# Dilated attention heads regrouped by residue modulo 4: 100 tile pairs a head in place of 136

## The chip, the cores and the metric

One core of one Trainium2 chip runs the whole program in one launch. The metric is the device time in microseconds (us), the median of the runs shown. The engines are TensorE (PE, with its weight loads listed as PEld), VectorE (DVE), ScalarE (ACT), GpSimd (POOL) and SyncE (SP, which issues most DMAs).

## What is computed

The reference is one inference step of a two-layer decoder trunk for a prompt of 2048 tokens and 8 samples of 4 tokens (T = 2048, 32 sample rows, D_MODEL 1024, heads of 128 columns, all fp32). Layer 0 has gated DeltaNet and retention heads. Layer 1 has 4 forgetting-attention heads (C) and 4 dilated ALiBi heads (D). The part that matters here is what a D head does to the prompt:

```python
D_BRANCHES = ((128, 1), (512, 4), (2048, 16))      # window, dilation
parts = [band_branch(dq, dk, dv, slopes, dil, win // dil) for win, dil in D_BRANCHES]
o_d = merge_branches(parts)     # one softmax over the keys of all three branches
# band_branch: s = q.k - slope * distance for distance = 0, dil, 2*dil, ... win, causal
o = concat([o_c * silu(cg), o_d * silu(dg)]);  y = o @ w_out;  x + y
```

So a query at position t sees every key at distance 0 to 128, every fourth key up to 512, and every sixteenth key up to 2048. A key that two or three branches hold counts two or three times. Everything beyond distance 128 lies at a distance divisible by 4, so on keys of the query's own residue modulo 4. `k` and `v` of the prompt are outputs too.

## The kernel before, in words

`build` runs stages one after another: tokens are loaded and turned, the heads of layer 0 (`heads_A`, `heads_B`), `output_projection`, then `odd_heads` (line 1433), then `finish` (line 1836), which does the attention of the samples and the last output projection. The change touches `shape_constants` (line 49) and `odd_heads` alone.

`odd_heads` has one in-order program for each engine, tied by semaphores, and each runs over the 8 heads `u`: four C, then four D. For a head the order written by hand is this:

- **Projection.** `project(u, at)` (L1554) is called for 20 values of `at` (4 matrices in 5 chunks of 416 tokens). DVE takes each chunk from PSUM into `Q` (L1680). `Q[:, 0]` holds the queries with the features on the partitions, `Q[:, 1]` the keys, `Q[:, 2]` the values, `Q[:, 3]` the gate. From `at > 3 * NC` on, `turn_kv(u, g)` (L1570) turns keys and values into rows and DVE keeps them in `ktok` and `vtok` (L1690).
- **Rows.** The prompt is 16 rows `i` of 128 queries. Row i has i + 1 key tiles, in chunks of up to G = 4 tiles (512 keys, one PSUM bank). A tile pair is one tile of 128 queries against one of 128 keys. A head has 1 + 2 + ... + 16 = 136 pairs in 40 chunks.
- **Scores.** `scores(u, i, ch)` (L1578): 128 queries stationary, up to 512 keys moving. An fp32 matmul stands as two MATMUL instructions in the trace.
- **Softening.** `soften` on DVE (L1708) adds the bias row, writes the scores to one of three row slots (`slots`, two in `sc`, one in `Q[:, 2]`, the values being in `vtok` by then) and takes the maximum. `maximum` (L1713, L1714) closes the row. `soft` on ACT (L1777) takes the exponential of the row in place and its sum.
- **Turning.** `turn` (L1592): each 128x128 tile of the row is transposed into PSUM bank 4 or 5. DVE copies chunks 0 and 1 to `wt` (L1746), ACT chunks 2 and 3 (L1804).
- **Weighing.** `weigh` (L1603): `wt` stationary, `vtok` moving, accumulated in bank 6 or 7. DVE divides (`otok`, L1752), PE turns the result (`turn_output`, L1612), and DVE multiplies it by the gate into `O` (L1758, semaphore `o_done`).

Elsewhere in the kernel, `finish` has eight transposes (L1966) whose source is read with a step of 4 fp32 elements, 16 bytes.

The rows are pipelined two ahead. The PE loop of a row is:

```python
for step in range(steps(i)):
    if i + 2 < TILES and step < n_chunks[i + 2]: scores(u, i + 2, step)
    if step == 0: pe.wait_ge(s["exp_done"], TILES * u + i + 1)
    if step < n_chunks[i]: turn(u, i, step)
    if 1 <= step <= n_chunks[i]: weigh(u, i, step - 1)
    if step == 1 and i: turn_output(u, i - 1)
```

DVE goes through the same steps: `soften(i + 2, step)`, the copy of chunk `step` of row i, at step 0 the division of row i - 1, at step 2 its product with the gate, at the end `maximum(i + 2)`. After row 3 comes `keep_sample` (L1697, L1699), which saves the samples' columns. ACT does `soft(i + 1)`, then its copies of row i.

The SP queue loads the bias of a head (`bias`, 2048 columns) when the scores of the head before are kept, then the weights of the next head, then stores keys, values and, when `o_done` says so, rows 0 to 13 and rows 14 and 15 of `O`. POOL multiplies each set of weights by the norm's gain when they have landed (L1522), which falls into the attention part of each head but the last.

Of the kernel before, what the change touches and what calls it, by code (L numbers as in the profile page):

```python
# [19 lines left out]
X = mybir.AxisListType.X  # L20
# [29 lines left out]
def shape_constants():  # L50
# [51 lines left out]
    m = np.arange(T)  # L102
    window = np.stack([bias(i[:, None] + (T - P) - m[None, :], h) for h in range(H)]).astype(f)
# [19 lines left out]
RET = 324  # L123

# [1308 lines left out]
def odd_heads(nc, k, io):  # L1433

    with ExitStack() as c:
# [15 lines left out]
        slots = [sc[:, 0, :], sc[:, 1, :], Q[:, 2, 0:T]]  # L1451
        names = ["fw_loaded", "fw_scaled", "f_ready", "f_taken", "f_act", "f_dve", "f_turned", "cols_ready", "f_stored", "cols_stored",
# [8 lines left out]
        def weights(u):  # L1461
# [4 lines left out]
        n_chunks = [i // G + 1 for i in range(TILES)]  # L1466
        first = [sum(n_chunks[:i]) for i in range(TILES)]
        in_chunk = lambda i, ch: min(G, i + 1 - G * ch)
        by_v, by_s = sum(min(n, 2) for n in n_chunks), sum(max(n - 2, 0) for n in n_chunks)
        CHUNKS = sum(n_chunks)  # L1470

        kept_by = lambda u, i, ch: ("wt_kept_v", by_v * u + sum(min(n, 2) for n in n_chunks[:i]) + ch + 1) if ch < 2 else \
            ("wt_kept_s", by_s * u + sum(max(n - 2, 0) for n in n_chunks[:i]) + ch - 1)
        steps = lambda i: max(n_chunks[i] + 1, n_chunks[i + 2] if i + 2 < TILES else 0, 3)
        stores = lambda u: 16 * sum(4 + (2 if branch == "C" else 2 * B) for branch, h in HEADS[:u])

# [4 lines left out]
        def _(sp):  # L1481
# [43 lines left out]
        def _(pe):  # L1525
# [32 lines left out]
            def turn_kv(u, g):  # L1558
# [5 lines left out]
                for which in range(2):  # L1564
# [6 lines left out]
                    last.then_inc(s["kv_turned"], 1)  # L1571

            def scores(u, i, ch):
                if i and ch < n_chunks[i - 1]:
                    pe.wait_ge(s["scores_kept"], CHUNKS * u + first[i - 1] + ch + 1)
                j, n = G * ch, in_chunk(i, ch) * P
                diag = HEADS[u][0] == "C" and ch == n_chunks[i] - 1
                last = pe.matmul(k.ps[ch][:, 0:n], Q[:, 0, i * P:(i + 1) * P], Q[:, 1, j * P:j * P + n], start=True, stop=not diag)  # L1578
                if diag:
                    last = pe.matmul(k.ps[ch][:, n - P:n], k.c("ident"), k.c("causal_bias"), start=False, stop=True)  # L1580
                last.then_inc(s["scores_made"], 1)

            def turn(u, i, ch):

                at = first[i] + ch
                if at >= 2:
                    i2 = i if ch >= 2 else max(x for x in range(i + 1) if first[x] <= at - 2)
                    name, count = kept_by(u, i2, at - 2 - first[i2])
                    pe.wait_ge(s[name], count)
                for jj in range(in_chunk(i, ch)):  # L1590
                    j = G * ch + jj
                    last = pe.transpose(k.ps[4 + at % 2][:, jj * P:(jj + 1) * P], slots[i % 3][:, j * P:(j + 1) * P], k.c("ident"))  # L1592
                last.then_inc(s["wt_made"], 1)

            def weigh(u, i, ch):

                name, count = kept_by(u, i, ch)
# [3 lines left out]
                for jj in range(in_chunk(i, ch)):  # L1601
                    j = G * ch + jj
# [869 lines left out]
```

## Time and profile before

| | us |
|---|---|
| median of 3 runs | 4541.89 (4537.42 to 4545.32) |
| the profiled execution | 4539.22 |
| its span, first to last instruction | 4537.4 |
| `odd_heads`, the four C heads | about 2101.8 to 2960 |
| `odd_heads`, the four D heads | about 2960 to 3812 |
| `finish` | about 3815 to the end |

Over the span PE is busy 91%, PEld 56%, DVE 38%, ACT 21% and POOL 3%; the mean granted TensorE clock is 0.951 of full speed. All times inside a profile are counted from the start of its span. The span is 1.8 us shorter than the execution's own time, and that execution is 2.7 us below the median. Each D head is a projection of about 124.5 us followed by an attention part of about 88 us. PE, DVE and ACT rows give busy time. An instruction that waits for a semaphore is not busy, and consecutive matmuls overlap: the start of one to the start of the next is what one costs.

### The profile page before, as it was taken

What the parts mean: (1) busy time and instruction counts of PE and PEld (TensorE: products, weight loads), DVE (VectorE), ACT (ScalarE), POOL (GpSimd) and SP (SyncE); (2) the same over time, 40 slices, a digit from 0 to 9 for tenths busy, and PEclk for the clock granted to TensorE, in tenths of its full rate; (3) what the DMA queues carried; (4) which work ended last, traced back from release to release, by engine and by line L of the source; (5) the groups of instructions that cost most, each with busy time, mean ns of one, the idle gap of its engine ahead of it and who ended that gap; (6) DMA issues with size and microseconds to landing.
All of it is one profiled execution on the core that took longest, in us unless ns stands there. A gap on an engine that the chain in (4) does not pass through costs nothing. (4 is left out here: it accounts for less than half of the span.)

```text
span 4537.4 us, 59156 instructions
## 1 busy us (share of the span) xinstructions
PE 4114.4 (91%) x23986; PEld 2525.4 (56%) x23986; DVE 1740.9 (38%) x3961; ACT 961.5 (21%) x1526; POOL 146.1 (3%) x67
## 2 busy tenths in 40 slices
PE   5899989999899999799999999999999997889896
PEld 2475665857555555454565666656565655444443
DVE  2364554647221222212334241515151425444442
ACT  2232332323110110112222222222222222000111
POOL 0000000000000000000000000000000000000000
PEclk7899999999899999899999999999999998999897
DMA  4001020100615523300101010101010102789886
GB/s 106 10 6 43 6 43 5 20 24 6 187 34 164 177 75 113 115 31 10 38 19 38 19 38 19 38 19 48 9 57 15 42 19 86 262 293 312 288 286 223
DMA packets 250756, 379.32 MB, mean 84 GB/s; under 512 B 23369, under 2 KB 154766, under 8 KB 247786
## 3 DMA queue, kind: packets, MB, share of 16 engines
q1 hardware_dynamic: 190358, 185.86, 14.5%
q10 hardware_dynamic: 51408, 157.31, 10.2%
q0 software_dynamic: 8720, 32.38, 2.1%
q8 instruction: 191, 3.13, 0.3%
q14 instruction: 79, 0.65, 0.0%
HBM read 327.90 MB, written 114.56 MB: 98 GB/s over the span
## 5 line engine op out<-in xcount | busy, mean ns | idle before, releaser
L475 PE MATMUL ps<-xT,big 128*128 128x416 f32 x2560 | 909.5, 517 | 15.6 <-PEq L143 9.4
L1554 PE MATMUL ps<-xT,big 128*128 128x416 f32 x2560 | 902.2, 512 | 0.0
L475 PEld LDWEIGHTS ps<-xT,big 128*128 128x128 f32 x2560 | 490.9, 192 | 431.2 <-issue 425.0
L1554 PEld LDWEIGHTS ps<-xT,big 128*128 128x128 f32 x2560 | 483.8, 190 | 397.0 <-issue 396.9
L1680 DVE TENSOR_TENSOR big<-ps,rstd 128x416 f32<-128x416 f32 x160 | 94.7, 592 | 801.1 <-PE ps L1554 801.1
L1603 PE MATMUL ps<-vtok,wt 128*128 128x128 f32 x2176 | 297.0, 280 | 31.9 <-DVE wt L1746 30.9
L2055 PE MATMUL ps<-o_words,big 128*128 128x512 f32 x512 | 286.2, 648 | 27.7 <-DVE xT L2203 13.9
L1578 PE MATMUL ps<-big 128*128 128x512 f32 (+3 forms) x640 | 289.7, 534 | 6.5 <-DVE vtok L1690 6.5
L1603 PEld LDWEIGHTS ps<-vtok,wt 128*128 128x128 f32 x2176 | 264.9, 192 | 53.8 <-DVE wt L1746 51.5
L1375 PE MATMUL ps<-big,wout 128*128 128x416 f32 x640 | 226.5, 516 | 19.1 <-DMA big<-scr_o 19.1
L2146 DVE STREAM_TRANSPOSE big<-rstd 128x512 f32<-128x512 f32 x312 | 207.1, 691 | 62.0 <-DMA rstd<-in_cache_fox_k 47.2
L490 DVE TENSOR_TENSOR big<-ps,rstd 128x416 f32<-128x416 f32 x100 | 59.1, 591 | 447.1 <-PE ps L475 446.9
L1777 ACT ACTIVATE sc<-sc,stat 128x128 f32<-128x128 f32 (+10 forms) x88 | 103.7, 1179 | 430.0 <-DVE stat L1714 430.0
L1375 PEld LDWEIGHTS ps<-big,wout 128*128 128x128 f32 x640 | 122.5, 192 | 122.5 <-issue 102.7
L1708 DVE CUSTOM_DVE_ANT_0 sc<-ps,bias 128x512 f32<-128x512 f32 (+3 forms) x216 | 130.3, 603 | 108.0 <-PE ps L1578 84.6
L1746 DVE COPY wt<-ps 128x512 f32<-128x512 f32 (+1 forms) x224 | 140.9, 629 | 34.4 <-PE ps L1592 34.4
L2029 PE MATMUL ps<-vring,big 128*4 128x128 f32 x2496 | 123.5, 286 | 30.1 <-issue 17.4
L1592 PEld LDWEIGHTS ps<-pack,sc 128*128 128x128 f32 x728 | 91.1, 142 | 80.2 <-issue 71.4
L2261 ACT COPY srow<-ps 128x1024 f32<-128x1024 f32 (+1 forms) x40 | 39.6, 991 | 438.5 <-PE ps L1990 438.5
L684 PE MATMUL ps<-big 128*128 128x128 f32 x896 | 130.9, 288 | 1.6 <-DVE grp L905 0.2
L2055 PEld LDWEIGHTS ps<-o_words,big 128*128 128x128 f32 x512 | 80.6, 194 | 92.1 <-issue 77.9
L2029 PEld LDWEIGHTS ps<-vring,big 128*4 128x4 f32 x2496 | 40.2, 84 | 162.8 <-issue 136.5
(403 smaller groups left out, 4690.9 us busy)
## 6 DMA issues: line engine op xcount, KB each, us to landing
rstd<-in_cache_fox_k SPq DMA_DIRECT2D x256, 256.0 KB, 4.2
vring<-in_cache_fox_v ACTq DMA_DIRECT2D x256, 256.0 KB, 4.5
out_win_k_sample<-in_cache_win_k ACTq DMA_DIRECT2D x8, 4088.0 KB, 28.8
out_win_v_sample<-in_cache_win_v ACTq DMA_DIRECT2D x8, 4088.0 KB, 40.7
big<-in_w_in_even SPq DMA_DIRECT2D x32, 512.0 KB, 10.7
big<-in_w_in_odd SPq DMA_DIRECT2D x32, 512.0 KB, 6.9
o_words<-scr_o POOLq DMA_DIRECT2D x8, 2048.0 KB, 11.5
rstd<-in_cache_win_k SPq DMA_DIRECT2D x56, 256.0 KB, 6.0
```

What stands on the lines that cost most here:

```text
L475: last = pe.matmul(k.ps[banks[at % 2]][:, 0:CH], k.w[:, j, m * P:(m + 1) * P], k.xT[:, j, n * CH:(n + 1) * CH], start=(j == 0), stop=(j == ...
L684: last = pe.matmul(dst, lhs[0:w, sl[i]], rhs[0:w, sl[i]], start=True, stop=True)
L1375: last = pe.matmul(k.ps[at % 4][:, 0:CH], wout[:, j, m * P:(m + 1) * P], o[:, n % 2, j, :], start=(j == 0), stop=(j == KT - 1))
L1554: last = pe.matmul(k.ps[PBANK[at % 2]][:, 0:CH], k.w[:, j, m * P:(m + 1) * P], k.xT[:, j, n * CH:(n + 1) * CH], start=(j == 0), stop=(j == ...
L1578: last = pe.matmul(k.ps[ch][:, 0:n], Q[:, 0, i * P:(i + 1) * P], Q[:, 1, j * P:j * P + n], start=True, stop=not diag)
L1603: last = pe.matmul(k.ps[6 + i % 2][:, 0:P], wt[:, (first[i] + ch) % 2, jj * P:(jj + 1) * P], vtok[:, j, :], start=(j == 0), stop=(j == i))
L1708: dve.tensor_tensor_reduce(slots[i % 3][:, j * P:j * P + n], k.ps[ch][:, 0:n], bias[:, at:at + n], 1.0, -3e38, ALU.add, ALU.max, cmax[:, i ...
L1746: dve.tensor_copy(wt[:, at % 2, 0:n], k.ps[4 + at % 2][:, 0:n]).then_inc(s["wt_kept_v"], 1)
L1777: act.activation(slots[i % 3][:, 0:n], slots[i % 3][:, 0:n], ACT.Exp, bias=stat[:, i % 3, 0:1], accum_out=stat[:, i % 3, 1:2]).then_inc(s[ ...
L2029: last = pe.matmul(k.ps[4][32 * hh:32 * hh + L, 0:P], weights[:, L * hh:L * hh + L], rows[:, hh * P:(hh + 1) * P], start=first, stop=final)
L2055: last = pe.matmul(k.ps[7], wout[:, unit, j, :], o[:, j, :], start=(j == 0), stop=(j == KT - 1))
L2146: dve.transpose(kt[:, at % 2, p % PAGES, :], kring[:, it % RING, :]).then_inc(s["k_turned"], 1)
```

## The change

Only the D heads change what they do. A row `i` is now the 128 queries of residue `i % 4` of the block of 512 tokens number `i // 4` (`tokens(u, i)`, a slice with step 4). It has one chunk or two:

- chunk 0 (near): the 512 keys of its own block, 4 tiles;
- chunk 1 (far, from row 4 on): for each earlier block its 128 keys of the same residue, but for the block just before, whose keys of that residue and whose last 128 keys in a row both stand. That is `i // 4 + 1` tiles.

The tiles of a head are 4 x 4 + 4 x 6 + 4 x 7 + 4 x 8 = 100, in 28 chunks. Score banks alternate between even and odd rows. The three row slots are 1024 wide and all lie in `sc`. Chunk 1 is copied by ACT, chunk 0 by DVE. In `turn_kv`, for g = 0, 1, 2, four more transposes turn the values by residue into bank 4, and DVE copies them to `Q[:, 2]`. The bias comes as two tables, `bias` (2048 columns) and `near` (515 columns, in `sc`), by two DMAs, and SP waits for `wt_made` of the head before as well. `O` is stored as rows 0 to 11 and 12 to 15. For the C heads the same functions give the same instructions as before, with that one more wait in SP.

```diff
+    window = np.zeros((H, P, WINDOW_COLS), f)       # WINDOW_COLS = T + 515
...
-        slots = [sc[:, 0, :], sc[:, 1, :], Q[:, 2, 0:T]]
...
+        TILES_OF = {"C": [[min(G, i + 1 - G * ch) for ch in range(i // G + 1)] for i in range(TILES)],
+                    "D": [[G] if i < G else [G, i // G + 1] for i in range(TILES)]}
+        by_act = lambda u, ch: ch >= (2 if HEADS[u][0] == "C" else 1)
...
+        steps = lambda u, i: max(n_chunks(u, i) + 1, n_chunks(u, i + 2) if i + 2 < TILES else 0, 3)
+        bank = lambda u, i, ch: ch if HEADS[u][0] == "C" else 2 * (i % 2) + ch
+        row_slots = {"C": [sc[:, 0, :], sc[:, 1, :], Q[:, 2, 0:T]],
+                     "D": [sc[:, 0, 0:T // 2], sc[:, 0, T // 2:T], sc[:, 1, 0:T // 2]]}
+        near = sc[:, 1, T // 2:T // 2 + 515]
+        def tokens(u, i):
+            if HEADS[u][0] == "C":
+                return slice(i * P, (i + 1) * P)
+            return slice(512 * (i // 4) + i % 4, 512 * (i // 4 + 1), 4)
...
                 if u:
-                    sp.wait_ge(s["scores_kept"], CHUNKS * u)
-                src = io.scr_f[h:h + 1, :].broadcast_to([P, T]) if fox else io.c_window[h:h + 1].rearrange("o p n -> (o p) n")
-                sp.dma_start(bias, src).then_inc(s["bias_loaded"], 16)
+                    sp.wait_ge(s["scores_kept"], before(u))
+                    sp.wait_ge(s["wt_made"], before(u))
+                if fox:
+                    sp.dma_start(bias, io.scr_f[h:h + 1, :].broadcast_to([P, T])).then_inc(s["bias_loaded"], 16)
+                else:
+                    sp.dma_start(bias, io.c_window[h, :, 0:T]).then_inc(s["bias_loaded"], 16)
+                    sp.dma_start(near, io.c_window[h, :, T:]).then_inc(s["bias_loaded"], 16)
...
-                for a, b in ((0, TILES - 2), (TILES - 2, TILES)):
+                for a, b in ((0, TILES - 2), (TILES - 2, TILES)) if fox else ((0, TILES - 4), (TILES - 4, TILES)):
...
+                if HEADS[u][0] == "D" and g < 3:          # in turn_kv, PE
+                    if g or u > H:
+                        pe.wait_ge(s["vs_kept"], 3 * (u - H) + g)
+                    for r in range(4):
+                        last = pe.transpose(k.ps[4][:, r * P:(r + 1) * P], Q[:, 2, 512 * g + r:512 * (g + 1):4], k.c("ident"))
+                    last.then_inc(s["vs_turned"], 1)
 
             def scores(u, i, ch):
+                fox = HEADS[u][0] == "C"
+                old = i - (1 if fox else 2)
+                if old >= 0 and ch < n_chunks(u, old):
+                    pe.wait_ge(s["scores_kept"], before(u) + first(u, old) + ch + 1)
+                out, q = k.ps[bank(u, i, ch)], Q[:, 0, tokens(u, i)]
...
+                elif ch == 0:
+                    at = 512 * (i // 4)
+                    last = pe.matmul(out, q, Q[:, 1, at:at + 512], start=True, stop=True)
+                else:
+                    at = 512 * (i // 4)
+                    pe.matmul(out[:, 0:n - P], q, Q[:, 1, i % 4:at:4], start=True, stop=True)
+                    last = pe.matmul(out[:, n - P:n], q, Q[:, 1, at - P:at], start=True, stop=True)
...
+            def values(u, i, ch, jj):
+                if HEADS[u][0] == "C":
+                    return vtok[:, G * ch + jj, :]
+                ab, r = divmod(i, 4)
+                if ch == 0:
+                    return vtok[:, 4 * ab + jj, :]
+                if jj == ab:
+                    return vtok[:, 4 * ab - 1, :]
+                return Q[:, 2, 512 * jj + r * P:512 * jj + (r + 1) * P]
...
+                if u >= H:                                # PE, before the rows
+                    pe.wait_ge(s["vs_kept"], 3 * (u - H + 1))
...
+                if HEADS[u][0] == "D" and g < 3:          # in keep_kv, DVE
+                    dve.wait_ge(s["vs_turned"], 3 * (u - H) + g + 1)
+                    dve.tensor_copy(Q[:, 2, 512 * g:512 * (g + 1)], k.ps[4]).then_inc(s["vs_kept"], 1)
...
-                at = j * P + (0 if HEADS[u][0] == "C" else T - (i + 1) * P)
+                if HEADS[u][0] == "C":                    # in soften, DVE
+                    add = bias[:, j * P:j * P + n]
+                elif ch == 0:
+                    add = near[:, 3 - i % 4:3 - i % 4 + n]
+                else:
+                    add = bias[:, 512 * (i % 4 + 1) - n:512 * (i % 4 + 1)]
...
-                            dve.tensor_tensor(O[:, (i - 1) * P:i * P], k.ps[6 + (i - 1) % 2][:, P:2 * P], Q[:, 3, (i - 1) * P:i * P],
+                            dve.tensor_tensor(O[:, tokens(u, i - 1)], k.ps[6 + (i - 1) % 2][:, P:2 * P], Q[:, 3, tokens(u, i - 1)],
                                               ALU.mult).then_inc(s["o_done"], 1)
...
-                    for ch in range(2, n_chunks[i]):
+                    for ch in range(n_chunks(u, i)):      # ACT
+                        if not by_act(u, ch):
+                            continue
```

## Rows read from the trace of the kernel before

**Rows 1.** The page: busy time, share of the span, instructions of each engine.

```profile
PE 4114.4 (91%) x23986; PEld 2525.4 (56%) x23986; DVE 1740.9 (38%) x3961; ACT 961.5 (21%) x1526; POOL 146.1 (3%) x67
```

**Rows 2.** Busy time by stretch: a projection, then the attention parts of four D heads.

```profile
core 0: us, PE busy (x) PEld busy (x) DVE busy (x) ACT busy (x) POOL busy (x), PEclk, DMA share, GB/s
3599.40:3723.90 124.50, 122.33 (x367) 66.84 (x366) 20.51 (x32) 23.68 (x27) 0.00 (x0) 1.00 0.03 10
3084.30:3173.10 88.80, 82.82 (x514) 62.10 (x515) 55.65 (x193) 25.98 (x42) 7.02 (x1) 0.98 0.20 59
3297.10:3385.20 88.10, 81.41 (x514) 61.46 (x515) 56.12 (x193) 25.98 (x42) 7.02 (x1) 1.00 0.20 59
3509.20:3599.90 90.70, 82.94 (x515) 62.34 (x515) 57.54 (x193) 25.98 (x42) 7.02 (x1) 0.98 0.20 58
3723.90:3811.50 87.60, 81.09 (x512) 61.09 (x512) 55.64 (x193) 25.98 (x42) 0.00 (x0) 1.00 0.12 36
```

**Rows 3.** Waits in the D heads: us in total, times, longest.

```profile
PE ps L1603 <- DVE wt L1746: 17.1, 28, 1.9
```

**Rows 4.** Timeline of PE, last D head: start, us, line, count, idle before.

```profile
3727.69 0.91 PE L1578 MATMUL ps<-big 128*128 128x384 f32 x2 [0.81 <-DVE vtok L1690]
...
3735.77 1.02 PE L1578 MATMUL ps<-big 128*128 128x512 f32 x2
...
3738.19 1.16 PE L1603 MATMUL ps<-vtok,wt 128*128 128x128 f32 x8 [0.52 <-DVE wt L1746]
3739.18 0.27 PE L1612 MATMUL ps<-pack,otok 128*128 128x128 f32 x1
3739.29 1.02 PE L1578 MATMUL ps<-big 128*128 128x512 f32 x2
...
3747.54 1.02 PE L1578 MATMUL ps<-big 128*128 128x512 f32 x2
3748.40 0.60 PE L1592 MATMUL ps<-pack,sc 128*128 128x128 f32 x4
3748.84 1.02 PE L1578 MATMUL ps<-big 128*128 128x512 f32 x2
...
3754.86 1.06 PE L1603 MATMUL ps<-vtok,wt 128*128 128x128 f32 x8
3755.75 0.27 PE L1612 MATMUL ps<-pack,otok 128*128 128x128 f32 x1
...
3798.38 1.04 PE L1592 MATMUL ps<-pack,big 128*128 128x128 f32 x8
3799.76 1.16 PE L1603 MATMUL ps<-vtok,wt 128*128 128x128 f32 x8 [0.35 <-DVE wt L1746]
...
3808.34 2.00 PE L1603 MATMUL ps<-vtok,wt 128*128 128x128 f32 x16
```

**Rows 5.** Timeline of DVE, last D head: the last product with the gate.

```profile
3811.22 0.29 DVE L1758 TENSOR_TENSOR big<-ps,big 128x128 f32<-128x128 f32 x1 [0.42 <-PE ps L1612]
```

**Rows 6.** Timeline of ACT, last D head: an exponential and a copy.

```profile
3747.47 1.15 ACT L1777 ACTIVATE sc<-sc,stat 128x1024 f32<-128x1024 f32 x1 [2.74 <-DVE stat L1714]
...
3807.21 0.59 ACT L1804 COPY wt<-ps 128x512 f32<-128x512 f32 x1 [4.01 <-PE ps L1592]
```

**Rows 7.** Timeline at half clock: contiguous scores, contiguous transposes, transposes with step 4.

```profile
3090.46 1.92 PE L1578 MATMUL ps<-big 128*128 128x512 f32 x2
3092.17 0.63 PE L1592 MATMUL ps<-pack,sc 128*128 128x128 f32 x2
...
3822.80 1.98 PE L1966 MATMUL ps<-pack,vring 128*128 128x128 f32 x8 [4.82 <-DMA vring<-in_cache_fox_logf,pages_col]
```

**Rows 8.** Timeline of the third D head: POOL's scaling of weights, DVE's `keep_sample`.

```profile
3520.12 7.02 POOL L1522 TENSOR_TENSOR big<-big,g_odd 128x4096 f32<-128x4096 f32 x1 [206.31 <-DMA big<-in_w_in_odd]
...
3525.30 2.04 DVE L1697 COPY wins<-big 128x32 f32<-128x32 f32 x3
```

**Rows 9.** DMA issues: count, KB each, median us to landing.

```profile
rstd<-in_cache_fox_k SPq DMA_DIRECT2D x256, 256.0 KB, 4.2
```

More of the change, by code:

```diff
@@ L123 @@
 RET = 324
+WINDOW_COLS = T + 515
 def window_rows():
@@ new lines, in odd_heads, with kept_by @@
+        pairs = [PAIRS[branch] for branch, h in HEADS]
+        before = lambda u: sum(len(p) for p in pairs[:u])
+        by_act = lambda u, ch: ch >= (2 if HEADS[u][0] == "C" else 1)
+        n_chunks = lambda u, i: len(tiles_of[u][i])
+        first = lambda u, i: pairs[u].index((i, 0))
+        def kept_by(u, at):
+            who = by_act(u, pairs[u][at][1])
+            earlier = [(v, ch) for v in range(u) for _, ch in pairs[v]] + [(u, ch) for _, ch in pairs[u][:at + 1]]
+            return "wt_kept_s" if who else "wt_kept_v", sum(by_act(v, ch) == who for v, ch in earlier)
@@ L1571, in turn_kv @@
                     last.then_inc(s["kv_turned"], 1)
-            def scores(u, i, ch):
[L1574 to L1580, printed above, removed]
+                if HEADS[u][0] == "D" and g < 3:
+                    if g or u > H:
+                        pe.wait_ge(s["vs_kept"], 3 * (u - H) + g)
+                    for r in range(4):
+                        last = pe.transpose(k.ps[4][:, r * P:(r + 1) * P], Q[:, 2, 512 * g + r:512 * (g + 1):4], k.c("ident"))
+                    last.then_inc(s["vs_turned"], 1)
@@ L1581, in scores @@
                 last.then_inc(s["scores_made"], 1)
             def turn(u, i, ch):
-                at = first[i] + ch
+                at = first(u, i) + ch
                 if at >= 2:
-                    i2 = i if ch >= 2 else max(x for x in range(i + 1) if first[x] <= at - 2)
-                    name, count = kept_by(u, i2, at - 2 - first[i2])
+                    name, count = kept_by(u, at - 2)
                     pe.wait_ge(s[name], count)
-                for jj in range(in_chunk(i, ch)):
+                for jj in range(tiles_of[u][i][ch]):
@@ L1600, in weigh @@
                     pe.wait_ge(s["otok_ready"], TILES * u + i - 1)
-                for jj in range(in_chunk(i, ch)):
-                    j = G * ch + jj
-                    last = pe.matmul(k.ps[6 + i % 2][:, 0:P], wt[:, (first[i] + ch) % 2, jj * P:(jj + 1) * P], vtok[:, j, :],
-                                     start=(j == 0), stop=(j == i))
-                if ch == n_chunks[i] - 1:
+                n, final = tiles_of[u][i][ch], ch == n_chunks(u, i) - 1
+                for jj in range(n):
+                    last = pe.matmul(k.ps[6 + i % 2][:, 0:P], wt[:, at % 2, jj * P:(jj + 1) * P], values(u, i, ch, jj),
+                                     start=(ch + jj == 0), stop=(final and jj == n - 1))
+                if final:
                     last.then_inc(s["o_made"], 1)
@@ L1738, in _ @@
                 for i in range(TILES + 1):
[L1739 to L1740 removed]
+                    for step in range(steps(u, i) if i < TILES else 3):
+                        if i + 2 < TILES and step < n_chunks(u, i + 2):
                             soften(u, i + 2, step)
[L1742 to L1745 removed]
+                        if i < TILES and step < n_chunks(u, i) and not by_act(u, step):
+                            at = first(u, i) + step
+                            n = tiles_of[u][i][step] * P
+                            dve.wait_ge(s["wt_made"], before(u) + at + 1)
                             dve.tensor_copy(wt[:, at % 2, 0:n], k.ps[4 + at % 2][:, 0:n]).then_inc(s["wt_kept_v"], 1)
```

69 lines of the change are left out of this document (35 added, 34 removed).

## The prediction, made before the changed kernel was run

> **What bounds the kernel now.** I read the page first: PE is busy 91% of the span, the other engines far less [rows 1]. Only D heads change, so I then cut that stretch into projection and attention. A D head's projection is 124.5 us at full clock, PE busy all but 2 us of it and DVE busy 20.5. Its attention part is 87.6 to 90.7 us, PE busy 81 to 83 and DVE 56 [rows 2]. So PE bounds both parts, and work taken from PE should show nearly whole, as long as no chain through DVE or ACT takes its place. The waits show how near such a chain is: PE's weighing waited 17.1 us in the four heads for DVE's copy of the transposed tiles, 28 times, so in early rows above all [rows 3]. Last I walked the rows of the last D head on PE's timeline [rows 4].
>
> **Price of a tile pair on PE,** from start to start [rows 4]. Scores: two matmuls of 512 columns from 3747.54 to 3748.40, 0.86 us for four tiles, 0.215 a tile. Turning: four transposes from 3748.40 to 3748.84, 0.44, so 0.109. Weighing: eight matmuls from 3754.86 to 3755.75, 0.89, so 0.223. Together 0.547 us a pair. 36 pairs fewer is 19.7 us a head; what replaces them decides the rest.
>
> **The floor of a row.** Call S0 the near scores of row i + 2, T0 and T1 the transposes of row i, W0 and W1 its weighing. When PE has little between S0 and W0, W0 waits for S0, then the softening, then the copy by DVE: S0 at 3735.77, W0 at 3738.19, 2.42 us. A W0 that has waited takes 0.99 (3738.19 to 3739.18), and turning the last output 0.11 (to 3739.29); this row took 3.52 [rows 4]. In the new D rows every near chunk has four tiles, so this floor holds in all of them. A row costs max(2.42, 0.86 + 0.44 + S1 + T1) + W0 + 0.11 + W1, with W0 0.99 after a wait and 0.89 without. The far chunk of n tiles has S1 0.215n, T1 0.109n, W1 0.223n.
> - Rows 0 to 3 (no far chunk): 3.41 for row 0, which has no output to turn, 3.52 for each other; 13.97.
> - Rows 4 to 7 (2 far tiles, and 2 or 3 scored ahead): PE reaches W0 at 1.95 or 2.16, under 2.42. 3.52 + 0.45 = 3.97 each; 15.88.
> - Rows 8 and 9 (3, scoring 3): 2.27, still under. 4.19 each. Rows 10 and 11 (3, scoring 4): 2.49, no wait, 4.16 each. Together 16.70.
> - Rows 12 and 13 (4, scoring 4): 2.60 + 1.00 + 0.89 = 4.49 each; 8.98.
> - Rows 14 and 15 score nothing. The W0 of such a row starts 1.38 after its first transpose (3798.38 to 3799.76). 1.38 + 0.99 + 0.11 + 0.89 = 3.37 each; 6.74.
> - Tail: the last weighing starts at 3808.34, 16 x 0.112 later is 3810.13 [rows 4], and the last product ends at 3811.51 [rows 5]: 1.38.
>
> Sum 63.65 us. The same stretch before is 3727.69 to 3811.51, 83.8 us [rows 4, 5]. Saved: 20.15 a head.
>
> **What is added in a head.** Twelve transposes of values beside the projection, 12 x 0.109 = 1.31. Row 0 scores four tiles in place of one there, 3 x 0.215 = 0.64. PE is full in that part, so both count [rows 2]. Row 1 scores four tiles in place of two just before the rows, and its softening is longer: 0.4 (bounds 0.3 to 0.7). Sum 2.35; net 17.8 a head, 71.2 for four.
>
> **At nothing.** Three more DVE copies a head, of the size of those DVE makes there, lie in a projection where DVE is busy 20.5 of 124.5 us [rows 2]. ACT takes far copies of 256 to 512 columns: each takes 0.59 at most [rows 6]. In row 14 weighing could start 1.38 - 0.44 = 0.94 after the last transpose, with a copy by DVE between; the same after T1 is covered by W0 and the output, 0.89 + 0.11 = 1.00. ACT's exponential of the next row, 1024 columns there as here, took 1.15 and began at 3747.47, as PE began its row at 3747.54 [rows 4, 6]. So it is over long before T1 ends, 1.95 to 2.6 into the row. DVE's product with step 4 takes 0.29 now [rows 5]; twice that would delay only an exponential needed a row later. In SP, the wait for `wt_made` stands behind a wait for `o_done` of the same head, which comes later; behind it are the bias loads (some 0.26 MB more for `near`) and the next weights. The bias is asked for a projection ahead, over 100 us; if that cover failed, a landing of some 4 us would show [rows 9]. The last store of `O` is 256 KB in place of 128 KB, open at the end of the stage: 0.3 us, bounds 0 and 4.2 [rows 9].
>
> **Disturbances before.** The attention parts of the other three D heads are 1.2, 0.5 and 3.1 us above the last one's [rows 2]. In the third, POOL scales weights from 3520.12 to 3527.14, and DVE's three copies of `keep_sample`, starting at 3525.30, took 2.04 in all and ended with POOL [rows 8]; half clock followed. PE's projection ended at 3509.2, so POOL ended 17.9 us after it. The new rows reach `keep_sample` some 4.2 + 13.97 = 18.2 us after the projection, where before it was 16.1. So it should come just behind POOL: 3.6 us back in two heads. The half clock of the first D head I leave.
> The Trainium skill ("SBUF — State Buffer", Who interferes with whom) says that a DVE copy using both ports and a GpSimd instruction exclude each other for the whole instruction. The trace agrees; if the order came out the other way, it would give those 3.6 us back and perhaps as much again.
>
> **The sum.** 71.2 + 3.6 - 0.3 = 74.5 us. The profiled execution took 4539.2, its span 4537.4; less 74.5 is 4464.7. It lay 2.7 below the median of 4541.9, so the median after is 4467.
>
> **Unknown: operands with step 4.** No matmul of this trace has its moving operand with a step. Below 1 time the contiguous price is excluded, as 0.427 us for 512 columns is already the full clock's pace. The nearest row above is the same matmul at half clock, two in 1.92 against 1.02, start to start twice as long [rows 4, 7]. For a stationary operand there is a row: at half clock two contiguous transposes take 0.63, so eight at twice 0.109 apart would take 0.63 + 6 x 0.218 = 1.94, and eight with step 4 took 1.98 [rows 7]. So the load costs nothing there, and I take 1 time for both. At full clock the twelve transposes could still be held at twice 0.109: 1.3 a head, 5 us.
>
> **Rivals.**
> 1. *The strided keys stream at half pace.* For: nothing in the trace shows full pace. Against: the free stationary loads [rows 7]. There are 24 such tiles a head, 0.215 more each. Rows 4 to 7 hide theirs under the 2.42; rows 8 and 9 pay 0.17 each, 10 and 11 0.28, 12 to 15 0.645: 3.5 a head, 13.9 in all, 4481. The Trainium skill ("Advanced Engine Details and Errata", SBUF Cachelines) says lines are 16 bytes, two hits on a line are needed to absorb latency, and a new line for each access is penalised. By that rule this rival holds; the transposes with step 4 do not bear it out.
> 2. *The ACT copy becomes the wait.* If the exponential of row i + 1 came in front of the far copy, W1 would wait up to 1.15 less the 0.06 to spare, 1.1 us, in twelve rows of four heads: 52 us given back, 4519. For: ACT has both jobs in one order. Against: it idles 62 of 88 us [rows 2].
> 3. *Slower.* Same place as rival 1, a larger price. With e more for each strided tile, a head pays 24e - 3.1, where 3.1 is what the waits for W0 hide: 0.69 in rows 2 and 3, 0.47 in 4 and 5, 0.26 in 6 and 7, 0.15 in 8 and 9. That eats 18.6 us from e = 0.90, a strided column at 5.2 times the contiguous price. Nothing seen is above 2 times.
>
> **How the numbers follow.** Forecast 0.77, rival 1 0.14, rival 2 0.06, rival 3 0.03. The first two cases make the range: 4455 (PE's own work alone saves 18.4 a head, and the clock holds throughout) to 4488 (rival 1, with the 5 us of slower transposes and 2 for a store or a second half-clock stretch). A measurement of this kernel tells 0.2% (9 us) from no change; all cases but the last are beyond it. Faster 0.96, same 0.01, slower 0.03.
>
> **What would show it.** Right: 100 tiles of scores, transposes and weighing a head, so 200 weighing MATMULs in place of 272; row starts 3.5 us apart in rows 1 to 3, 4.0 in 4 to 7, 4.2 in 8 to 11, 4.5 in 12 and 13; attention part about 68 us and projection part about 126.5; the same C heads; DVE's `keep_sample` copies at 0.17 each. Rival 1: score matmuls of 128 to 384 columns starting further apart than 0.107 per 128. Rival 2: PE waiting at W1 for `wt` from ACT. Wrong as a whole: row starts above 4.5 us throughout, or granted clock falling in each D head.

## The result, and the profile after

| | before | after |
|---|---|---|
| median of 4 runs | 4541.39 us (4537.42 to 4545.32) | 4492.44 us (4489.57 to 4495.72) |
| profiled execution, its span | 4539.2, 4537.4 | 4494.2, 4492.4 |
| stretch of the four D heads | 851.8 | 805.2 |

The ratio is 0.9892, 95% interval 0.9875 to 0.991: faster by 49 us, where 74.5 were forecast. Of the 45.0 us between the two profiled executions, 46.6 lie in the stretch of the four D heads; the stretch ahead of them took 1.8 less and the one behind them 3.3 more. The runs that follow show up to 4 us between kernels with the same code in the first of these, and up to 13 in the second (720.4 to 733.4), so I argue from the D stretch alone.

The page after, its busy times [rows 1]:

```profile
PE 4079.9 (91%) x23602; PEld 2521.3 (56%) x23602; DVE 1704.5 (38%) x3829; ACT 945.0 (21%) x1526; POOL 146.9 (3%) x67
```

PE has 384 instructions fewer, 96 a head: 36 pairs with one transpose and two weighing matmuls each are 108, less the 12 transposes of values. The work went as the diff says. But PE's busy time fell by 34.5 us only.

Busy time by stretch after: the projection of the last D head, then the attention parts of the first and the last D head; the two between are as the first [rows 2].

```profile
core 0: us, PE busy (x) PEld busy (x) DVE busy (x) ACT busy (x) POOL busy (x), PEclk, DMA share, GB/s
3561.50:3688.20 126.70, 124.55 (x379) 68.81 (x378) 22.88 (x35) 23.98 (x27) 0.00 (x0) 1.00 0.04 13
3084.70:3159.80 75.10, 69.94 (x407) 57.84 (x407) 45.55 (x157) 21.69 (x42) 7.02 (x1) 1.00 0.23 68
...
3688.20:3763.30 75.10, 69.48 (x405) 57.42 (x404) 45.55 (x157) 21.69 (x42) 0.00 (x0) 1.00 0.13 40
```

The projection part is 126.7 (forecast 126.5). The attention part is 75.1 in every head, at full clock, where about 68 was forecast. So the miss is 7 us a head, the same in all four, inside the attention part, and PE is busy through it: no new wait. The waits of PE confirm that; the column is the total, the number of times and the longest [rows 3]:

```profile
PE ps L1663 <- DVE wt L1816: 10.4, 16, 1.0
```

The wait for DVE's copy fell from 17.1 us in 28 places to 10.4 in 16. What grew is on PE's timeline, two stretches of the last D head [rows 4]; L1625 scores the near chunk, L1628 the far tiles with a step of 4 in the keys, L1629 the last tile of the far chunk, L1640 turns, L1663 weighs:

```profile
3699.80 1.14 PE L1625 MATMUL ps<-big 128*128 128x512 f32 x2
3700.78 0.60 PE L1640 MATMUL ps<-pack,sc 128*128 128x128 f32 x4
3701.21 0.72 PE L1628 MATMUL ps<-big 128*128 128x128 f32 x2
3701.76 0.55 PE L1629 MATMUL ps<-big 128*128 128x128 f32 x2
3702.34 1.16 PE L1663 MATMUL ps<-vtok,wt 128*128 128x128 f32 x8
...
3703.44 1.14 PE L1625 MATMUL ps<-big 128*128 128x512 f32 x2
...
3744.00 1.14 PE L1625 MATMUL ps<-big 128*128 128x512 f32 x2
3744.98 0.60 PE L1640 MATMUL ps<-pack,sc 128*128 128x128 f32 x4
3745.42 1.62 PE L1628 MATMUL ps<-big 128*128 128x384 f32 x2
3746.86 0.51 PE L1629 MATMUL ps<-big 128*128 128x128 f32 x2
3747.20 0.60 PE L1640 MATMUL ps<-pack,sc 128*128 128x128 f32 x4
3747.64 1.06 PE L1663 MATMUL ps<-vtok,wt 128*128 128x128 f32 x8
3748.53 0.27 PE L1672 MATMUL ps<-pack,otok 128*128 128x128 f32 x1
3748.64 0.83 PE L1663 MATMUL ps<-big,wt 128*128 128x128 f32 x6
...
3749.54 1.14 PE L1625 MATMUL ps<-big 128*128 128x512 f32 x2
```

In the short row (3.64 us, forecast 3.52) the near scores take 0.98 from start to start, not 0.86, and the floor from S0 to W0 is 2.54, not 2.42. In the long row (5.54, forecast 4.49) the near scores are again 0.12 longer and the far chunk takes 1.78 from 3745.42 to 3747.20, where four tiles were priced 0.86; turning (0.44), weighing (0.89 and 0.90) and the output (0.11) are as forecast. So every score matmul that reads an operand with a step of 4 is dearer, and nothing else in the row is. The near scores have contiguous keys: there only the queries, which PE loads as weights, have the step.

The groups by shape show both sides; columns: busy us, mean ns of one | idle before. After, the loads and the matmuls of the scores:

```profile
L1625 PEld LDWEIGHTS ps<-big 128*128 128x128 f32 x128 | 34.8, 320 | 6.0 <-DVE vtok L1752 6.0
L1628 PE MATMUL ps<-big 128*128 128x384 f32 x32 | 26.0, 902 | 0.0
L1628 PE MATMUL ps<-big 128*128 128x256 f32 x32 | 18.8, 678 | 0.0
```

Before, in the same view:

```profile
L1578 PEld LDWEIGHTS ps<-big 128*128 128x128 f32 x640 | 97.5, 193 | 8.0 <-DVE vtok L1690 8.0
L1578 PE MATMUL ps<-big 128*128 128x384 f32 x64 | 26.8, 500 | 6.5 <-DVE vtok L1690 6.5
L1578 PE MATMUL ps<-big 128*128 128x256 f32 x64 | 19.1, 380 | 0.0
```

A load of queries went from 193 to 320 ns. A moving column went from (500 - 380) / 128 = 0.94 ns (0.83 by start to start) to (902 - 678) / 128 = 1.75 ns.

DVE's last product with the gate now has a step too, 0.38 for 0.29 [rows 5]; ACT's exponential of 1024 columns took 1.15 as before and its copy of 512 columns 0.58 for 0.59 [rows 6], no wait of PE on ACT appeared, and a 256 KB load landed in 4.3 us, 4.2 before [rows 9]. The last product of the last D head on DVE:

```profile
3762.88 0.38 DVE L1828 TENSOR_TENSOR big<-ps,big 128x128 f32<-128x128 f32 x1 [0.42 <-PE ps L1672]
```

POOL's scaling and DVE's sample copies met before, in the third D head [rows 8]. After they stand apart in all; the first D head:

```profile
3095.39 7.02 POOL L1554 TENSOR_TENSOR big<-big,g_odd 128x4096 f32<-128x4096 f32 x1 [209.69 <-DMA big<-in_w_in_odd]
```

```profile
3104.34 0.34 DVE L1762 COPY wins<-big 128x32 f32<-128x32 f32 x3
```

POOL ends at 3102.41, the copies start 1.93 us later and take 0.34 in all. No D head shows a half clock.

### The profile page after: what moved, and what is told of

It is laid out like the page before. It is cut to its first block and busy times, and to the rows that moved or that the text cites. A ratio compares the mean times of both kernels' runs of the same rounds, so it can differ in the third digit from the quotient of the medians.

```text
span 4492.4 us, 58269 instructions
## 1 busy us (share of the span) xinstructions
PE 4079.9 (91%) x23602; PEld 2521.3 (56%) x23602; DVE 1704.5 (38%) x3829; ACT 945.0 (21%) x1526; POOL 146.9 (3%) x67
## 5 line engine op out<-in xcount | busy, mean ns | idle before, releaser
L1663 PE MATMUL ps<-vtok,wt 128*128 128x128 f32 x1696 | 237.2, 280 | 24.5 <-DVE wt L1816 24.0
L1663 PEld LDWEIGHTS ps<-vtok,wt 128*128 128x128 f32 x1696 | 208.9, 192 | 37.8 <-DVE wt L1816 37.0
L1847 ACT ACTIVATE sc<-sc,stat 128x512 f32<-128x512 f32 (+11 forms) x108 | 113.5, 1051 | 458.8 <-DVE stat L1784 458.8
L1620 PE MATMUL ps<-big 128*128 128x512 f32 (+3 forms) x320 | 143.8, 531 | 3.3 <-DVE vtok L1752 3.3
L2062 PE MATMUL ps<-big,qrep 32*32 32x256 f32 (+1 forms) x5120 | 129.8, 448 | 3.7 <-issue 3.6
L1640 PEld LDWEIGHTS ps<-pack,sc 128*128 128x128 f32 x764 | 98.4, 147 | 58.4 <-issue 49.0
L1816 DVE COPY wt<-ps 128x512 f32<-128x512 f32 (+3 forms) x176 | 114.3, 649 | 23.6 <-PE ps L1640 23.6
```

What stands on the lines that cost most here:

```text
L1620: last = pe.matmul(out[:, 0:n], q, Q[:, 1, j * P:j * P + n], start=True, stop=not diag)
L1663: last = pe.matmul(k.ps[6 + i % 2][:, 0:P], wt[:, at % 2, jj * P:(jj + 1) * P], values(u, i, ch, jj), start=(ch + jj == 0), stop=(final an ...
L1816: dve.tensor_copy(wt[:, at % 2, 0:n], k.ps[4 + at % 2][:, 0:n]).then_inc(s["wt_kept_v"], 1)
L1847: act.activation(row, row, ACT.Exp, bias=stat[:, i % 3, 0:1], accum_out=stat[:, i % 3, 1:2]).then_inc(s["exp_done"], 1)
L2062: last = pe.matmul(k.ps[row][32 * hh:32 * hh + 32, 0:n * 32], qrep[lane, f, j, hh, :], kt[lane, at % 2, 0:n, (4 * hh + j) * 32:(4 * hh + j ...
```

## The experiments

**Theory A:** operands with a step of 4 cost PE time at full clock, keys and queries each. **Rival B:** the rows are longer because of the new order (longer S0 and softening, the floor of a row wrongly read). First series: three kernels take the step away, from the far keys, from the queries, from both, and one halves it. "Attention" below is a D head from the end of its last projection matmul to its last product with the gate, as in the windows above; the changed kernel has 75.1.

| kernel | median us (range of 4) | ratio to before [95%] | attention | D stretch |
|---|---|---|---|---|
| e1_keys | 4477.57 (4476.74 to 4487.94) | 0.9866 [0.985, 0.9882] | 70.9 | 788.5 |
| e2_queries | 4477.73 (4471.78 to 4481.02) | 0.9855 [0.9839, 0.9872] | 71.6 | 791.1 |
| e3_both | 4468.18 (4464.95 to 4471.11) | 0.9838 [0.9821, 0.9854] | 68.2 | 777.3 |
| e4_step2 | 4479.06 (4472.16 to 4483.54) | 0.9857 [0.9841, 0.9874] | 71.0 | 789.2 |
| e5_step3 | 4484.3 (4481.03 to 4489.1) | 0.9864 [0.9847, 0.988] | 72.9 | 796.8 |

**e1_keys,** contiguous far keys (of other tokens):

```diff
-pe.matmul(out[:, 0:n - P], q, Q[:, 1, i % 4:at:4], start=True, stop=True)
+pe.matmul(out[:, 0:n - P], q, Q[:, 1, 0:n - P], start=True, stop=True)
```

> The changed kernel, but the far scores of a D row read as many keys in a row from the start of the head's keys, in place of every fourth key, so the far scores are of other keys. Theory A, that the missing gain is paid on PE where operands have a step of 4: the far matmuls fall from about 1.78 ns a column to 0.83; a chunk of 4 tiles should take about 1.1 us in place of 1.79, one of 3 about 0.9 in place of 1.34, and rows 6 to 13 get shorter until the 2.4 to 2.5 us wait for the copy holds them. Attention part of a D head 75.1 to about 70.6 us, 18 us off the whole, about 4474. Theory B, that the rows are held by the chain through DVE and ACT and the slow matmuls lie under it: the attention part stays at 75 and the time at 4492.

**e2_queries,** contiguous queries (other tokens), keys as in the change:

```diff
-out, q = k.ps[bank(u, i, ch)], Q[:, 0, tokens(u, i)]
+out, q = k.ps[bank(u, i, ch)], Q[:, 0, i * P:(i + 1) * P]
```

> The changed kernel, but the scores of a D row take 128 queries in a row as the stationary operand in place of every fourth of 512, so the queries are others. Theory A: weight loads of the scores fall from 0.31 to 0.19 us, the near scores of a row from 0.98 to 0.86 us, each far chunk by 0.1 or so; the attention part falls by about 2 us a head, the whole by 8 to 9, about 4484. Theory B: no change, 4492.

**e3_both,** both edits:

> Both at once: queries and far keys of the scores read in a row. Theory A: scores cost 0.215 us a tile again, and each row takes what the forecast said: attention part about 68 us a head, the whole about 29 us less than the changed kernel, 4464 to 4467, so the sum of the two single edits or a little more. Theory B: no change. If the attention part ends clearly above 68, the forecast's floor of a row was wrong as well.

**e4_step2,** the far keys with a step of 2, `Q[:, 1, i % 4:i % 4 + 2 * (n - P):2]`:

> The far scores read every second key (8 bytes apart) in place of every fourth (16 bytes apart), so they are of other keys; the queries keep their step of 4. Theory A1, what costs is that each element lies in another 16 bytes: step 2 is as fast as no step, the time is that of the run with keys in a row, about 4474. Theory A2, any step costs: the far matmuls stay at 1.78 ns a column and the time at 4492.

Read the table in pairs. With contiguous queries (e2_queries) the strided keys still cost 71.6 - 68.2 = 3.4 us a head; with contiguous keys (e1_keys) the strided queries cost 70.9 - 68.2 = 2.7; both together 6.9. Theory A holds, and B falls: with both steps gone and the order kept, the head is back at 68.2, and its rows are 3.52 in rows 1 to 3, 3.97 in 4 to 7 (4.03 in row 4) and 4.19 in 8 to 11, within 0.06 of the forecast. A long row of e3_both on PE's timeline, to be read against the 5.54 us row above:

```profile
3720.01 1.02 PE L1625 MATMUL ps<-big 128*128 128x512 f32 x2
3720.87 0.60 PE L1640 MATMUL ps<-pack,sc 128*128 128x128 f32 x4
3721.30 0.81 PE L1628 MATMUL ps<-big 128*128 128x384 f32 x2
3721.95 0.38 PE L1629 MATMUL ps<-big 128*128 128x128 f32 x2
3722.17 0.60 PE L1640 MATMUL ps<-pack,sc 128*128 128x128 f32 x4
...
3724.50 1.02 PE L1625 MATMUL ps<-big 128*128 128x512 f32 x2
```

Far chunk 0.87, row 4.49. The same chunk is 1.11 us in e1_keys and 1.58 in e2_queries: of the 0.91 above 0.87 in the changed kernel, 0.24 are what is left exposed of the loads of strided queries, and 0.71 are three tiles of strided keys, 0.237 a tile (together they overlap by 0.04).

A step of 2 (8 bytes) is nearly free, 71.0 for 70.9. That left open how the price depends on the step, which **e5_step3** asks, `Q[:, 1, i % 4:i % 4 + 3 * (n - P):3]`:

> The changed kernel with its far keys taken at every third token instead of every fourth (12 bytes apart instead of 16), so the scores of the far keys are of other tokens; count and shapes of all instructions stay. With step 4 a D head's attention takes 75.1 us, with step 1 70.9, with step 2 71.0. Theory A1 (each 16-byte line costs two columns' time, so a step of 3 costs 1.5 times, three lines for four elements): 73.0 us, a 128x384 matmul of the far scores about 0.68 us where step 4 shows 0.90. Rival A2 (a threshold: any step of 16 bytes or more costs double, below it nothing): 71.0 us and 0.46 us. Rival A3 (any step over 8 bytes costs double): 75.1 us and 0.90 us.

The far scores by shape, columns as above, in e5_step3, then e4_step2 (in e1_keys, step 1, it is 547 ns); the queries have the step of 4 in all three:

```profile
L1628 PE MATMUL ps<-big 128*128 128x384 f32 x32 | 20.7, 733 | 0.0
L1628 PE MATMUL ps<-big 128*128 128x256 f32 x32 | 15.3, 564 | 0.0
```

```profile
L1628 PE MATMUL ps<-big 128*128 128x384 f32 x32 | 15.5, 566 | 0.0
```

72.9 us against A1's 73.0: it is neither a threshold at 16 bytes nor one above 8. The column costs (733 - 564) / 128 = 1.32 ns: 3/4 of the 1.75 with a step of 4, as three 16-byte lines hold four elements at a step of 3. Half of 1.75 would be 0.88 with a step of 2, which is nearly the contiguous 0.83. My 0.68 us for one matmul was too low (0.73), as the exposed load adds to it. So the Trainium skill's rule ("Advanced Engine Details and Errata", SBUF Cachelines: two hits on a 16-byte line are needed) is what the trace shows at steps of 2, 3 and 4 for float32.

**The disturbance that the change removed: e6_keep.** I had put the uneven heads of before down to DVE's sample copies meeting POOL's scaling. Edit:

```diff
-                    if i == 3:
+                    if i == 2:
                         keep_sample(u)
```

> The changed kernel with one thing moved: DVE copies a head's sample columns after row 2 instead of after row 3, some 4 us earlier. In the trace of the changed kernel those copies start 1.93, 2.65, 2.99 us after GpSimd's 7.02 us scaling of the weights has ended (first three D heads; the fourth has no scaling), and all four heads take 75.1 us. Theory (the disturbance that the change took away is a DVE copy that meets GpSimd's scaling and is held until it ends): the copies now meet it with about 2.1, 1.4 and 1.1 us of it to go, the first copy lasts that long instead of 0.17 us, and the heads take about 77.0, 76.4, 76.0 and 75.1 us: 3.5 to 4.5 us more in all. Rival (the two only stood beside each other, and the disturbance of before came from the low clock of the matmuls there): all copies stay at 0.17 us, four heads of 75.1 us, total unchanged.

Measured: 4518.91 us (4512.95 to 4520.53), 0.9944 [0.9927, 0.996]: 26 us above the changed kernel, not 4. The D heads took 78.4, 75.7, 75.6 and 75.0, so 4.6 us more in all before rounding, about what the theory said, though less evenly. The other 21 us are in the C heads, whose `keep_sample` the same line moves; I had left them out. They took 94.8, 96.3, 94.3 and 94.6 where the changed kernel has 89.5, 90.5, 89.5 and 89.5; the first sample copy took 2.4 to 4.6 us in each, until POOL's scaling ended, and half clock followed. The first D head of before is another matter: its copies start 0.4 us behind POOL's end, at 17.2 us after the projection, and its 1.2 us go with the half clock of [rows 7], which stands ahead of them. First D head of e6_keep, DVE and POOL:

```profile
3123.44 2.36 DVE L1762 COPY wins<-big 128x32 f32<-128x32 f32 x3
```

```profile
3118.57 7.02 POOL L1554 TENSOR_TENSOR big<-big,g_odd 128x4096 f32<-128x4096 f32 x1 [215.03 <-DMA big<-in_w_in_odd]
```

POOL ends at 3125.59, and the first of the three copies, 0.17 us of work, with it. PE then:

```profile
3127.19 1.53 PE L1663 MATMUL ps<-vtok,wt 128*128 128x128 f32 x8 [1.99 <-DVE wt L1816]
...
3128.73 1.91 PE L1625 MATMUL ps<-big 128*128 128x512 f32 x2
3130.44 0.99 PE L1640 MATMUL ps<-pack,sc 128*128 128x128 f32 x4
3131.27 0.68 PE L1628 MATMUL ps<-big 128*128 128x128 f32 x2
```

```profile
3127.80:3132.10 4.30, 4.30 (x16) 3.18 (x16) 2.06 (x9) 1.03 (x2) 0.00 (x0) 0.60 0.00 0
3128.73:3130.44 1.71, 1.71 (x4) 0.59 (x4) 0.60 (x3) 0.80 (x1) 0.00 (x0) 0.50 0.00 0
3131.27:3131.76 0.49, 0.49 (x4) 0.49 (x3) 0.40 (x3) 0.00 (x0) 0.00 (x0) 1.00 0.00 0
```

PE waited 1.99 us for the copy of the turned weights, which stood behind the sample copies, and after that gap the granted clock is 0.60 on average for 4.3 us (PEclk in the last three rows, which are of the windows view), at its lower level (1.2 GHz) for most of it. So a hold of 2.2 us cost the head 3.3. These rows also answer why half clock told me nothing of strided loads: near scores with strided queries take 1.71 here (3128.73 to 3130.44, granted clock 0.50), and contiguous ones took 1.71 at half clock before [rows 7]. The strided far tile behind them (3131.27 to 3131.76) ran at full clock again. So no run here shows a strided moving operand at half clock.

**Versions that keep the result and take the steps away.** Second series, each on top of the one before it:

| kernel | median us (range of 4) | ratio to before [95%] | attention, D heads | attention, C heads |
|---|---|---|---|---|
| f1_regroup | 4462.35 (4460.45 to 4468.95) | 0.9816 [0.98, 0.9833] | 68.2 68.3 68.2 68.2 | 89.7 90.3 89.6 89.5 |
| f2_turn_first | 4449.74 (4447.3 to 4455.79) | 0.9788 [0.9772, 0.9805] | 64.8 63.4 63.6 62.9 | 89.6 90.6 89.8 89.5 |
| f3_all_heads | 4445.78 (4442.71 to 4452.56) | 0.9786 [0.977, 0.9803] | 64.6 63.6 63.5 62.9 | 89.3 91.7 89.3 89.4 |
| g1_keep5 | 4436.85 (4432.7 to 4440.55) | 0.9764 [0.9747, 0.978] | 62.7 in each | 87.3 in each |

**f1_regroup:** DVE writes the queries by residue as it takes them from the projection, and one copy puts the keys by residue.

```diff
+# take, queries of a D head, for each part of a block of 512
+dst = Q[:, 0, 512 * b:512 * (b + 1)].rearrange("p (r i) -> p i r", r=4)[:, (t0 - 512 * b) // 4:(t1 - 512 * b) // 4, :]
+last = dve.tensor_tensor(dst, src.rearrange("p (i r) -> p i r", r=4), k.rstd[:, t0:t1].rearrange("p (i r) -> p i r", r=4), ALU.mult)
+# after the keys are normed
+dve.tensor_copy(kres, Q[:, 1, 0:1536].rearrange("p (n r) -> p r n", r=4)).then_inc(s["kres_ready"], 1)
-pe.matmul(out[:, 0:n - P], q, Q[:, 1, i % 4:at:4], start=True, stop=True)
+pe.matmul(out[:, 0:n - P], q, kres[:, i % 4, 0:n - P], start=True, stop=True)
```

> The same work as the changed kernel, with contiguous operands for every score matmul: DVE writes the queries of a D head regrouped by residue as it takes them from the projection (nothing added, only its output's order), and one more DVE copy per D head (128x1536) puts the keys by residue into a buffer of their own; the far scores read that. Theory A (step-4 operands of TensorE are what the forecast lacked, both the far keys as moving operand and the queries as loaded weights): D heads' attention 68.2 us instead of 75.1, as where both were contiguous but the wrong tokens; the added copy takes about 1.6 us of DVE before row 4 and is hidden by the first rows; the total 75.1 to 68.2 four times is 27.6 us less than the changed kernel: 4465 us. Rival 1 (DVE pays for the order: the takes with a regrouping write are slower and hold back the projection): the projection part grows from 126.7 to 129 or more, the total stays at 4475 or above. Rival 2 (the copy of the keys comes late): row 4's first far scores wait for it, attention 69.5 to 71.

The head is 68.2 and the projection part 126.6: DVE's regrouping is hidden, neither rival came.

**f2_turn_first:** in D heads PE turns row i before it scores row i + 2, and DVE copies before it softens.

```diff
 for step in range(steps(u, i)):
+    early = step == 0 and u >= H
+    if early:
+        pe.wait_ge(s["exp_done"], TILES * u + i + 1)
+        turn(u, i, step)
     if i + 2 < TILES and step < n_chunks(u, i + 2):
         scores(u, i + 2, step)
```

> As f1_regroup, and in the D heads TensorE turns row i's first chunk before it scores row i+2, and DVE copies the turned weights before it softens row i+2. Theory (rows 0 to 11 of a D head keep a wait of TensorE for DVE's copy of the turned weights, because its softening of the next row stands in front of it): the wait goes, a row is then TensorE's own sum (3.52 to about 3.1 in rows 0 to 3, about 0.9 less in the later ones), attention 62 to 64 us instead of 68.2, total 4440 to 4450. Rival (DVE is the bound once its copy is no longer behind the softening: its softening now comes later, so ACT's exp comes later, and TensorE waits for that instead): attention 67 to 69, total within 5 us of f1_regroup, and the waits move from the weigh line to the turn line.

**f3_all_heads:** the same order in the C heads (`early = step == 0`).

> As f2_turn_first, with the same order in the C heads too (attention of 89.5 us per head before and after the change). Theory: the C heads hold the same wait of TensorE for the copy of the turned weights, 2 to 3 us per head; attention of a C head 86 to 88 us, total 6 to 14 us below f2_turn_first. Rival: C heads' score rows are long enough that the exp comes last, and turning first makes TensorE wait for it: C head 90 to 95 us, total above f2_turn_first.

**g1_keep5:** f3_all_heads with `keep_sample` after row 5.

> As f3_all_heads, with DVE's copies of the sample columns after row 5 instead of row 3. In f3_all_heads the heads in which these copies meet GpSimd's scaling take 64.6, 63.6 and 63.5 us in place of the last head's 62.9, and the second C head 91.7 in place of 89.3. Theory (the same hold of the copies): every D head 62.8 to 63.0, every C head 89.2 to 89.5, 5 to 6 us less than f3_all_heads: about 4440 us. Rival (these heads are longer for another reason): heads unchanged, total within 2 us of f3_all_heads.

In f2_turn_first the wait of the early rows goes, and rows 1 to 3 of the last D head take 2.88, not 3.52. But shorter rows brought the sample copies forward again, into POOL's scaling, and the first three heads paid 1.9, 0.5 and 0.7 for it. f3_all_heads looked like a failure: three C heads of 89.3 or 89.4, one of 91.7 (the 4 us between the medians lie in no head). With the copies after row 5 every D head is 62.7 and every C head 87.3, where I had expected 89.2 to 89.5. Was that the order or the copies? **h1_keep5_only** is f1_regroup with the copies after row 5 and the old order; **h2_strided** takes g1_keep5's regrouping away again and so prices the steps where no wait hides them.

> f1_regroup with the sample copies after row 5 and the order of turning as it was: with f3_all_heads (the order alone) and g1_keep5 (both) it tells which of the two is worth what in the C heads (f1_regroup 89.6 us, f3_all_heads 89.4 in three of four, g1_keep5 87.3). Theory A (order and copies hide each other: each alone gives nothing): C heads 89.4 to 89.6, D heads 68.2, total within 3 us of f1_regroup's 4462. Rival B (the copies alone were worth the 2 us, the order nothing in a C head): C heads 87.3 to 87.8, total 4453 to 4456.

> The changed kernel, its operands with a step of 4 as they are, with g1_keep5's order and sample copies. In the changed kernel the wait for DVE's copy hid a part of the steps' cost (6.9 us a head of it showed). Here nothing hides it. Theory (each strided near chunk costs 0.12 us, each strided far chunk 0.24 for its loads and 0.237 for each tile of keys): 16 x 0.12 + 12 x 0.24 + 24 x 0.237 = 10.5 us a head on top of g1_keep5's 62.7, so attention 72.5 to 73.5 us, C heads 87.3, total 4478 to 4482. Rival (the steps cost 6.9 a head whatever the order, as they run beside the waits): attention 69.6, total about 4465.

h1_keep5_only: 4462.92 us (4459.28 to 4468.74), 0.9819 [0.9803, 0.9835], C heads 89.5, 89.5, 89.5 and 90.8, D heads 68.1 or 68.2. In the fourth C head the granted clock is 0.50 for 3.4 us (2875.81 to 2879.22), ahead of the copies. So in a C head the order alone gives nothing (f3_all_heads), the copies alone 0.8 us in the second head and at most 0.2 in the first and third, and both together 2.1 us or more. The traces say why. Where the copies come late in both kernels, the order is worth 2.2 us (h1_keep5_only 89.5, g1_keep5 87.3). In f3_all_heads the shorter rows bring the first sample copy to 14.8 us after the projection, from 16.5 in f1_regroup, well inside POOL's scaling. It takes 2.0 us in three C heads and 3.0 in the second, and that gives the gain back. The first C head of f3_all_heads, DVE and POOL:

```profile
2244.21 2.21 DVE L1783 COPY foxs<-big 128x32 f32<-128x32 f32 x3
```

```profile
2239.19 7.02 POOL L1555 TENSOR_TENSOR big<-big,g_odd 128x4096 f32<-128x4096 f32 x1 [353.19 <-DMA big<-in_w_in_odd]
```

h2_strided: 4468.19 us (4466.91 to 4469.11), 0.9832 [0.9816, 0.9849], D heads 71.2: the steps cost 71.2 - 62.7 = 8.5 us a head, between the rival's 6.9 and my 10.5. More than 6.9, as the wait for DVE's copy had hidden some of it. Less than 10.5, as a far chunk that directly follows the near one has less of its loads exposed: with three tiles it takes 1.23 here (3708.43 to 3709.66), and 1.34 in the changed kernel. Twelve chunks at 0.11 are 1.3 of the 2.0 us missing; what the other 0.7 is stays open. The row of h2_strided on PE's timeline, then DVE's sample copies in the first D head of f3_all_heads and of g1_keep5:

```profile
3708.43 1.07 PE L1628 MATMUL ps<-big 128*128 128x256 f32 x2
...
3709.66 0.49 PE L1640 MATMUL ps<-pack,sc 128*128 128x128 f32 x3
```

```profile
3103.96 2.09 DVE L1783 COPY wins<-big 128x32 f32<-128x32 f32 x3
```

```profile
3098.80 0.34 DVE L1783 COPY wins<-big 128x32 f32<-128x32 f32 x3
```

g1_keep5 beats both kernels: 107 us under before, 56 under the changed one. PE's waits for DVE's copy in its D heads are down to 2.8 us from 10.4, and in row 2 no idle time is put down ahead of the weighing (2.88 us from row to row, 3.64 in the changed kernel):

```profile
PE ps L1664 <- DVE wt L1841: 2.8, 8, 0.3
```

```profile
3652.55 1.02 PE L1626 MATMUL ps<-big 128*128 128x512 f32 x2
...
3653.85 1.06 PE L1664 MATMUL ps<-vtok,wt 128*128 128x128 f32 x8
...
3655.43 1.02 PE L1626 MATMUL ps<-big 128*128 128x512 f32 x2
```

## Why the prediction missed

The direction was right and the size wrong: 49 us gained, 74.5 forecast, and 4492 lies above the range's 4488.

**The step that failed** is "Unknown: operands with step 4", in the words "So the load costs nothing there, and I take 1 time for both". Two things were wrong in it.
- The row that decided it stood at half clock [rows 7]. It showed that a strided load costs nothing there, and I carried that to full clock. At full clock a strided load of queries takes 320 ns for 193, and a strided column 1.75 ns for 0.83. e6_keep shows the difference on one and the same matmul: near scores with strided queries take 1.71 at half clock, as contiguous ones do, and 0.98 for 0.86 at full clock. For a strided moving operand there was no row at all, and the load's price was taken for it too. The text named this danger for the twelve transposes of values only (5 us) and not for the scores.
- The queries were taken as covered by "both" and then priced in no rival. Rival 1 had the strided keys at half pace: 3.5 us a head, 13.9 in all, 4481. e2_queries, where the keys alone have the step, measured nearly that: 3.4 a head and 4477.7. The strided queries added 2.7 alone and 3.5 on top of the keys (75.1 - 71.6), 14 us in four heads, for which the range had no room.

So the budget of the D stretch closes: forecast -71.2 - 3.6 = -74.8; e3_both, without the steps, 777.3 - 851.8 = -74.5; the changed kernel 27.9 more, of which 4 x 6.9 = 27.6 is the two steps. That forecast and e3_both agree to 0.3 is partly luck. The last head, which had no disturbance, gained 19.4 in its attention part and lost 2.0 in its projection, 17.4 net where 17.8 was forecast; the first got back 1.2 that the forecast had left aside.

**Right, by its own steps.**
- The price of a pair, the floor of a row (2.42 to W0, 3.52 the row) and the table of rows: e3_both and f1_regroup have these rows (4.19 for 4.16 in rows 10 and 11). In the changed kernel 0.12 of strided loads came on top of the floor.
- The added work beside the projection: 126.7 for 126.5. The transposes of values with a step load their weights in 210 ns for 140, and nothing of it shows in the projection part, so the bound of 5 us was not used.
- The disturbances: 3.6 us forecast, and before's heads were 1.2, 0.5 and 3.0 above the last one, 4.7 in all; none is left. The copies were forecast 18.2 us after the projection and came at 19.6, POOL ended at 17.7 for 17.9. e6_keep shows that this was a narrow pass: 4 us earlier, and the loss is 26 us. The text's price for the other outcome, "those 3.6 us back and perhaps as much again", was right for the D heads and looked at them alone.
- ACT's copies: no wait on them (rival 2 did not come). Rival 3 needed 5.2 times; 2.1 was measured.
- The range's low end, 4455, does not follow from the words beside it: 18.4 a head in place of 17.8 is 2.4 us, and the half clock of the first D head 1.2, so about 4464. Nothing hung on it.
- The end of the stage, 0.3 for the last store: the stretch behind the D heads is 3.3 us longer, but it varies by more than that between kernels with the same code there, so no run here shows it.

**The weight given.** Rival 1 had a chance of 0.14 with one row against it, and that row was at the other clock. "No matmul of this trace has its moving operand with a step" should have made it near to even, and the rule of 16-byte lines that the prediction takes from the Trainium skill ("Advanced Engine Details and Errata", SBUF Cachelines) spoke for it.

## What to carry to other kernels

For PE, price both operands by the bytes from element to element. For a float32 moving operand at full clock a step of 2 was nearly free, a step of 3 cost half as much again and a step of 4 double. For the operand loaded as weights only a step of 4 was tried: 320 ns for 193. Let the engine that writes the tile anyway write it regrouped, which cost nothing to see here. Do not carry a price read at half clock to full clock. And when rows get shorter, ask where the small DVE copies land against POOL's long instructions: a copy of 0.17 us can hold DVE for what is left of 7 us, PE waits behind it, and the clock falls after the wait.

## What the runs showed that I had not expected

- Strided float32 loads of weights are slow too, 320 ns for 193. Each pass of a float32 matmul has its own load, and part of it shows: 0.12 us on every near chunk and 0.24 on a far one. The cost of a step also depends on what surrounds it: 6.9 us a head in one order of the same work, 8.5 in another.
- At the lower clock strided loads of weights cost nothing: the near scores took 1.71 us there with and without the step. Strided columns were never seen at that clock.
- Moving one group of small copies by one row cost 26 us in 4492, 21 of them in heads that the change never touched.
- In C heads the new order alone gave nothing, as it moved the sample copies deeper into POOL's scaling; with the copies after row 5 it gave 2.2 us a head.
